# Attention scores of an encoder trunk: the rotary product on 128 partitions with the chunk mask in it, and output-projection products between the last attention steps

## What is computed

```python
q = jnp.concatenate([q[..., :NOPE_DIM],
                     apply_rope(q[..., NOPE_DIM:], cos[:, :, None, :], sin[:, :, None, :])], axis=-1)
...
def attend(args):
    qb, qc = args
    s = jnp.einsum('bqhd,bkhd->bhqk', qb, k).astype(jnp.float32) * scale
    mask = k_chunk[None, :] <= qc[:, None]
    s = jnp.where(mask[None, None], s, neg)
    p = jax.nn.softmax(s, axis=-1).astype(v.dtype)
    return jnp.einsum('bhqk,bkhd->bqhd', p, v)
...
return o @ w_o
```

## Time and profile before

| | us |
|---|---|
| median of 3 runs | 1961.33 (1961.1 to 1962.72) |
| span of the profiled execution, first to last instruction | 1960.5 |
| PE busy in it | 1873.7 (96%) |
| DVE busy | 998.9 (51%) |
| ACT busy | 590.6 (30%) |
| POOL busy | 266.5 (14%) |
| mean granted clock of PE, share of full speed | 0.973 |

### The profile page before, as it was taken

How to read it: one execution, slowest core, us unless ns; L and a number is a source line. 1 busy time by engine, 2 the same in 40 slices (tenths; PEclk the granted TensorE clock), 3 DMA queues, 4 the chain that set the end, 5 groups by cost and what they waited for, 6 DMA issues and landing times.

```text
span 1960.5 us, 22646 instructions
## 1 busy us (share of the span) xinstructions
PE 1873.7 (96%) x8196; PEld 1494.7 (76%) x8196; DVE 998.9 (51%) x1306; ACT 590.6 (30%) x794; POOL 266.5 (14%) x171
## 2 busy tenths in 40 slices
PE   8887999998999999999999999999899999999996
PEld 5665887785888888888878888888655778888885
DVE  7889358725645544442285444323744354444224
ACT  5122222222233332331153323212424342323213
POOL 7456105301301300000020000000200100000001
PEclk8999999999999999999999999999969999999998
DMA  4244425565632222222222222222100122222221
GB/s 161 92 142 139 137 97 164 152 250 176 195 123 96 97 96 96 96 97 96 97 86 96 96 96 96 97 97 96 65 22 1 65 97 96 96 96 96 97 96 54
DMA packets 79398, 207.93 MB, mean 106 GB/s; under 512 B 24576, under 2 KB 32896, under 8 KB 77296
## 3 DMA queue, kind: packets, MB, share of 16 engines
q1 hardware_dynamic: 75440, 187.86, 28.5%
q0 software_dynamic: 2752, 17.24, 2.6%
q10 hardware_dynamic: 1152, 2.10, 0.3%
HBM read 184.10 MB, written 23.07 MB: 106 GB/s over the span
## 4 chain that ended last, share of the span: by engine, by line
PE 80%; DVE 12%; issue 4%; ACT 2%; POOL 1%; DMA 0%; DVEq 0%; SPq 0%; ACTq 0%; POOLq 0%
PE bank L1356 24%; PE bank L1358 24%; PE bank L1357 23%; DVE w_split L912 2%; PE bank L1670 1%; PE bank L1669 1%; DVE h_split L932 1%; PE bank L1691 1%; ACT w_split L604 1%; DVE gate L925 1%; PE bank L1552 1%; PE bank L1559 1%; PE bank L1673 1%; PE bank L1388 1%; PE bank L1682 1%
## 5 line engine op out<-in xcount | busy, mean ns | idle before, releaser
L912 DVE TENSOR_TENSOR w_split<-w_raw,w_split 128x1024 fp32r<-128x1024 f32 x302 | 390.5, 1297 | 684.2 <-ACT w_split L604 679.0
L1356 PE MATMUL bank<-h_split,w_split 128*128 128x512 f32 x1488 | 586.4, 394 | 21.2 <-DVE gate L923 13.3
L1357 PE MATMUL bank<-h_split,w_split 128*128 128x512 f32 x1488 | 581.5, 391 | 0.0
L1358 PE MATMUL bank<-h_split,w_split 128*128 128x512 f32 x1488 | 581.3, 391 | 0.0
L604 ACT ACTIVATE w_split<-w_raw 128x1024 fp32r<-128x1024 f32 x302 | 316.5, 1055 | 723.7 <-PE bank L1358 719.7
L1356 PEld LDWEIGHTS bank<-h_split,w_split 128*128 128x128 f32 x1488 | 281.1, 189 | 87.8 <-DVE gate L923 11.9
L1356 PE MATMUL bank<-g_split,w_split 128*128 128x512 f32 (+1 forms) x856 | 335.8, 392 | 7.0 <-DVE gate L923 3.6
L1357 PE MATMUL bank<-g_split,w_split 128*128 128x512 f32 (+1 forms) x856 | 334.7, 391 | 0.0
L1358 PE MATMUL bank<-g_split,w_split 128*128 128x512 f32 (+1 forms) x856 | 334.5, 391 | 0.0
L1358 PEld LDWEIGHTS bank<-h_split,w_split 128*128 128x128 f32 x1488 | 280.8, 189 | 59.1
L1357 PEld LDWEIGHTS bank<-h_split,w_split 128*128 128x128 f32 x1488 | 281.0, 189 | 58.8 <-issue 1.0
(11 more groups left out here) (243 smaller groups left out, 1254.2 us busy)
## 6 DMA issues: line engine op xcount, KB each, us to landing
w_raw<-wstream SPq DMA_DIRECT2D x302, 512.0 KB, 3.2
op_slots<-s_ops POOLq DMA_DIRECT2D x5, 2048.0 KB, 8.3
s_ops<-ops_out SPq DMA_DIRECT2D x8, 1024.0 KB, 4.4
op_slots<-s_ops SPq DMA_DIRECT2D x3, 2048.0 KB, 8.3
s_ops<-c_pow POOLq DMA_DIRECT2D x8, 512.0 KB, 4.2
s_ops<-k_window SPq DMA_DIRECT2D x64, 64.0 KB, 3.3
x_res<-xT SPq DMA_DIRECT2D x8, 256.0 KB, 8.2
bc_in<-bcd POOLq DMA_DIRECT2D x8, 256.0 KB, 5.5
```

The costliest lines, as they stand in the source:

```text
L912: tt(W[:, r, 1, :], RAW[:, r, :], W[:, r, 0, :].bitcast(F32), ALU.subtract).then_inc(s_lo, 1)
L1356: mm(bank, hi, x_hi, start=start, stop=True, skip_group_check=True)
L1357: mm(bank, hi, x_lo, start=False, stop=True, skip_group_check=True)
L1358: return mm(bank, lo, x_hi, start=False, stop=True, skip_group_check=True)
```

## The change

The kernel after contracts all 128 partitions in the rotary product. The query tile, now `q_rope_and_rows`, has a place of its own for each of the 8 heads: one half of the partitions holds the head's rotary queries, the other half holds four rows that are 1 for the first 64 queries of tile t (and 60 rows of zeros). The key side has two tiles: `k_rope` for even heads and the former `c_kv` for odd ones (`KRP`), with the rotary key in one half and in the other four rows of -3e38 at the keys to be hidden. So L1673 falls away. POOL loads these rows with four transfers from a new 2 x 64 x 512 input and copies half of the key once. The product that ended with the mask now ends a step. DVE writes the rotary queries with two additions of 64 partitions in place of one of 128. The probabilities lie packed in 1280 columns per head. At the end of the attention, the first three projection packs are multiplied by heads 0 to 5 ahead of and between the last turns, and by heads 6 and 7 behind `values(7)`.

```diff
-                tt(QR[:, q, :], BK[ea % 8][:], COS[:], ALU.mult).then_inc(s_ev_v, 1)
+                tt(ACC[:], BK[ea % 8][:], COS[:], ALU.mult).then_inc(s_ev_v, 1)
                 wait_product(dve, eb)
                 tt(GT[:], BK[eb % 8][:], SIN[:], ALU.mult).then_inc(s_ev_v, 1)
                 wait_read(dve, eb)
-                tt(QR[:, q, :], QR[:, q, :], GT[:], ALU.add).then_inc(s_qr, 1)
-                dve.wait_ge(s_qr, q + 1)
+                for par in range(2):
+                    side = slice(64 * par, 64 * par + 64)
+                    tt(QR[side, 2 * q + par, :], ACC[side, :], GT[side, :], ALU.add).then_inc(s_qr, 1)
+                dve.wait_ge(s_qr, 2 * q + 2)
...
             sum_squares(N_KV)
+            pool.wait_ge(s_used, FFN1A + 3 * FT)
+            for par in range(2):
+                side = slice(64 * (1 - par), 64 * (1 - par) + 64)
+                pool.dma_start(QR[side, par:HEADS:2, :], mask[0].unsqueeze(1).broadcast_to([64, HEADS // 2, SEQ])
+                               ).then_inc(s_rows, 16)
             sum_squares(N_DQ)
+            pool.wait_ge(s_cs_lo, 1)
+            pool.wait_ge(s_sum, (SUMS[N_DQ] + 1) * (DT - 1))
+            nc.gpsimd.tensor_copy(CN[64:P, :], KR[64:P, :]).then_inc(s_kro, 1)
+            pool.wait_ge(s_kro, 1)
+            for par in range(2):
+                side = slice(64 * (1 - par), 64 * (1 - par) + 64)
+                pool.dma_start(KRP[par][side, :], mask[1]).then_inc(s_rows, 16)
...
-            pe.wait_ge(s_qr, 4)
+            pe.wait_ge(s_qr, HEADS)
+            pe.wait_ge(s_rows, 16 * 4)
...
                 n = P * (t + 1)
-                q0 = 64 * (h % 2)
                 mm(BK[t][:, 0:n], QN[:, h, t * P:(t + 1) * P], KN[:, h, 0:n], start=True, stop=True, skip_group_check=True)
-                mm(BK[t][:, 0:n], QR[q0:q0 + 64, h // 2, t * P:(t + 1) * P], KR[q0:q0 + 64, 0:n],
-                   start=False, stop=True, skip_group_check=True)
-
-                mm(BK[t][:, n - 64:n], MASK[0:1, 0:P], MASK[0:1, P:P + 64], start=False, stop=True,
+
+                mm(BK[t][:, 0:n], QR[:, h, t * P:(t + 1) * P], KRP[h % 2][:, 0:n], start=False, stop=True,
                    skip_group_check=True).then_inc(s_scores, 1)
...
-            for h in range(HEADS + 2):
+            def wo_part(d, heads):
+                for k in heads:
+                    pe.wait_ge(s_o_lo, k + 1)
+                    last = three(BK[d][:], *tile(WO + d, k), H[:, k, 0, :], H[:, k, 1, :], k == 0)
+                return last
+
+            for h in range(HEADS):
                 for t in range(4):
-                    if h < HEADS:
-                        scores(h, t)
-                    if 1 <= h <= HEADS:
+                    scores(h, t)
+                    if h >= 1:
                         turn(h - 1, t)
                     if t == 1 and h >= 2:
                         values(h - 2)
-            for d in range(DT):
+            early, last_two = range(HEADS - 2), range(HEADS - 2, HEADS)
+            values(HEADS - 2)
+            for d in range(AHEAD):
                 pack(WO + d)
-                if d in (4, 6, 7):
-
-                    pe.wait_ge(s_o_lo, HEADS)
-                column(WO + d, BK[d], H, (lambda k: pe.wait_ge(s_o_lo, k + 1)) if d == 0 else None)
+                pe.wait_ge(s_exp, 4 * (HEADS - 1) + d + 1)
+                wo_part(d, early)
+                if d < 2:
+                    turn(HEADS - 1, 2 * d)
+                    turn(HEADS - 1, 2 * d + 1)
+            values(HEADS - 1)
+            for d in range(AHEAD):
+                wo_part(d, last_two).then_inc(s_used, 1)
+            for d in range(AHEAD, DT):
+                pack(WO + d)
+                if d == 3:
+                    pe.wait_ge(s_exp, 4 * HEADS)
+                if d in (4, 5):
+                    pe.wait_ge(s_pt, 4 * HEADS)
+                column(WO + d, BK[d], H)
```

More of the change, by code:

```diff
@@ L135, in build @@
     EYE = at("eye", [P, P], F32, o_c + 800)
-    MASK = at("mask_rows", [1, P + 64], F32, o_c + 1312)
     STAT = at("attn_stat", [P, 32], F32, o_c + 2080)
@@ L190, in build @@
     QN = at("q_nope", [P, HEADS, SEQ], F32, o_g + 32 * K)
-    QR = at("q_rope", [P, 4, SEQ], F32, o_g + 48 * K)
-    PT = at("probs_t", [P, 2, 4, SEQ], F32, o_g + 56 * K)
-    PR = at("probs", [P, 2, 4, SEQ], F32, o_g + 72 * K)
+    QR = at("q_rope_and_rows", [P, HEADS, SEQ], F32, o_g + 48 * K)
+    PT = at("probs_t", [P, 2, 4, SEQ], F32, o_g + 64 * K)
+    PR = [at("probs_even", [P, 1280], F32, o_g + 80 * K), at("probs_odd", [P, 1280], F32, o_s + 2 * K)]
+    PR_AT = [0, 128, 384, 768]
+    KRP = [KR, CN]
     CS = at("c_kv_split", [P, 2, SEQ], F32R, o_g + 72 * K)
@@ L316, in wait_read @@
             eng.wait_ge(s_ev_v, [MSTAT, *range(MCQ, MID)].index(m) + 1)
-    CONSTS = 4
+    CONSTS = 3
     def in_turns(eng, stage, turn):
@@ L372, in reduced, with probs @@
         return ts(to_cos, to_cos, float(np.pi / 2), None, ALU.add)
+    def probs(h, t, first, end):
+        return PR[h % 2][:, PR_AT[t] + first:PR_AT[t] + end]
     with nc.Block() as block:
@@ L515, in _ @@
             pool.dma_start(EYE[:], consts[1]).then_inc(s_const, 16)
-            pool.dma_start(MASK[:], mask).then_inc(s_const, 16)
             pool.dma_start(DS[:], dskip).then_inc(s_const, 16)
@@ L844, in soft @@
                     act.wait_ge(s_tp, i - 7)
-                nc.scalar.activation(PR[:, h % 2, t, 0:n], BK[t][:, 0:n], ACT.Exp, bias=STAT[:, 4 + t:5 + t],
+                nc.scalar.activation(probs(h, t, 0, n), BK[t][:, 0:n], ACT.Exp, bias=STAT[:, 4 + t:5 + t],
                                      scale=QK_SCALE, accum_out=STAT[:, 8 + t:9 + t]).then_inc(s_exp, 1)
@@ L1681, in turn @@
                 for a in range(t + 1):
-                    last = nc.tensor.transpose(BK[4 + t % 2][:, a * P:(a + 1) * P],
-                                               PR[:, h % 2, t, a * P:(a + 1) * P], EYE[:])
+                    last = nc.tensor.transpose(BK[4 + t % 2][:, a * P:(a + 1) * P], probs(h, t, a * P, (a + 1) * P), EYE[:])
                 last.then_inc(s_tp, 1)
@@ L1779 @@
     consts = np.stack([np.ones((P, P), f), eye, np.roll(eye, 64, 0)])
-    mask = np.concatenate([np.repeat([1.0, 0.0], 64), np.full(64, NEG)]).astype(f)[None]
+    mask = np.zeros((2, 64, SEQ), f)
+    for t in range(4):
+        mask[0, t, t * P:t * P + 64] = 1.0
+        mask[1, t, t * P + 64:(t + 1) * P] = NEG
     def states(v):
```

4 lines of the change are left out of this document (2 added, 2 removed).

## The result

The kernel after takes **1937.77 us** (median of 4 runs, 1933.79 to 1937.82) against 1961.63 for the kernel before (4 runs beside them): a ratio of **0.9877**, 95% interval 0.9865 to 0.9889, 23.9 us faster. The forecast was 1932.4 in a range of 1927 to 1941.

The account below looks back on a forecast made before the run. PE, busy for 96% of the 1960.5 us span, was taken to bound the kernel. Terms 2.4 - 19.8 + 3.7 - 15.1 - 0.1 = -28.9 us gave 1931.6 from the span, 1932.4 from the median; range 1927 to 1941.

Parts of the forecast that it names:

- Term 1: Start of the scores: two 64-partition DVE additions replace one, 4 more operations at 0.60 us, +2.4 us.
- Term 2: Score steps: mask product and delays around products on few partitions go from 32 steps, -19.8 us.
- Term 3: Score loop: with shorter steps PE waits for ACT's copy of turned probabilities, in six heads and head 1, +3.7 us.
- Term 4: PE's clock in heads 0 to 2: low for about 5 us instead of through most of them, -15.1 us.
- Term 5: Tail from last scores to projection: new waits of 1.95 and 0.9 us replace 2.95 us of waits, -0.1 us.
- Cost nothing: POOL's row transfers, its key copy and one small load fewer at the start: no effect on the time.
- The delays stay: Rival, score steps: delays come from new accumulation or unhidden weight loads, not changing partitions; 1939 us, chance 0.12.
- The clock comes back late: Rival, first heads: scores don't raise the clock, half speed up to and with head 2's first values; 1944 us, chance 0.08.
- The clock low throughout: Rival: half clock through the whole score loop, to the first projection product; 1988 us, slower than before, chance 0.02.
- The softmax becomes the bound: Rival, score loop: the softmax chain is late by another microsecond in seven heads, +7; 1939 us, chance 0.06.
- PE's first score released by the mask rows: Sign of a wrong forecast at the first score: PE waits there for the mask rows instead of DVE.

Follow-up runs that it names:

- turn_later: Kernel after with each head's second turn and the values behind it moved behind the third scores instead of the second; 1931.22 us, ratio 0.9855.
- no_mask: Kernel before without its mask product (L1673), so the chunk mask is left out; 1940.59 us, ratio 0.9898.
- third_product: Kernel after with a one-partition product of 64 columns, adding zeros, at the end of each score step; 1948.64 us, ratio 0.9937.
- tail_only: Kernel before with only the loops at the end of the attention as the kernel after has them; 1961.37 us, ratio 1.0004.
- copy_by_dma: Kernel after with POOL's copy of half the rotary key made a transfer, and it and two mask-row transfers moved behind L600; 1933.94 us, ratio 0.9859.
- all_four: all_three plus the edit of turn_later, on the kernel after; POOL's transfers stand behind its four rotary additions; 1931.25 us, ratio 0.9854.
- after_again: Kernel after, unchanged, run again to see how its runs spread; 1936.70 us, ratio 0.9876.
- all_three: Kernel after with copy_by_dma's and pool_adds' edits, plus tail products reordered to cover the waits at the values of heads 6 and 7; 1934.99 us, ratio 0.9874.
- pool_adds: Kernel after with the odd head's rotary addition of each pair moved from DVE to POOL, products double-buffered; 1932.99 us, ratio 0.9852.
- scores_only: Kernel after with its new scores, but the end of the attention as in the kernel before; 1935.51 us, ratio 0.9863.

## Why the prediction was right, point by point

The forecast's mechanism held, the sign and the range too; the time was 5.3 us above the point. Two of its terms were each off by 2 us or more in opposite directions, which the sum hides.

- **Term 1** (+2.4) was mis-sized. Two 64-partition additions do cost as much as two of 128, but a pair of heads got 0.72 us longer, not 0.60: the second addition starts 0.72 us behind the first, as if it depended on it, though neither reads what the other writes. Why, no run shows. That is the upper bound, 2.9; PE's idle time grew by 2.99, to 5.22, outside the 4.4 to 4.8 that were to show the forecast right.
- **Term 2** (-19.8) was mis-sized: -22.3, beyond its own bound of -20.8. A head without a wait takes 7.57 us (turn_later), 2.82 less than 10.39. The steps follow at the pure stream, 0.86 and 0.22, so the whole 0.65 went from each of the 32 steps (-20.8), and the 0.03 left per step for a boundary don't exist. The rest, 1.5 us, is the 0.05 per turn that the forecast kept in its 1.31 us for the turns of a head. no_mask shows the mask's 0.36 go whole. By the Trainium skill (TensorE: Matmul & The Clock Gate, Back-to-back issue gap) the masks would be 1.6 us in all, by the prediction's estimate. no_mask alone gained 20.8 us by the medians, 11.5 of them by the row and most of the rest, 8.5, by the clock that came back 17 us earlier (an estimate: half of 17). (The prediction's -10.9 for the term by that figure leaves out the 1.0 it left for boundaries.)
- **Term 3** (+3.7) was mis-sized: the waits, 0.97 in head 1 and 0.57 in six heads, show as 4.4 us, but cost 5.7 by the starts, 1.13 in head 1 and 0.76 in each other. The reading of ACT's chain gave 0.45, taken as 0.5, and 0.7. turn_later confirms whose wait the 0.57 was. Terms 2 and 3 together came to -16.6 for -16.1: that the score stretch agrees to a tenth is luck.
- **Term 4** (-15.1): head 0 took 7.17 us for 4.32 at full clock (four steps of two products at 0.216 per 128 columns), so 2.85 for the 2.5 forecast: -14.8. The clock came back 5.6 us behind the first score, in head 0, for the 5 forecast. The reason was read too narrowly, though: `values` isn't what raises the clock, since it came back ahead of any `values` in no_mask and third_product too.
- **Term 5** (-0.1) **failed**: +1.57, outside its bounds of -2.0 and +1. The two waits came as forecast, 1.99 for 1.95 and 0.72 for 0.9, and tail_only measured -0.18 for the same code. What was left out is that the clock may fall behind a wait of 2 us: `values(6)` alone took 1.14 us more. The forecast had noted that 2.23 us of idle time ahead of the scores were followed by a fall, and did not apply it to the wait it was adding itself.
- **"Cost nothing" failed in part**: POOL's addition L600 was on time, as said, but its copy and the two transfers run beside DVE's splits, which take 0.4 us longer with them, and a second clock fall, behind the norm product's wait, came with it. The stretch to the first score lost 2.0 us beyond term 1. copy_by_dma moves the fall and does not prove its cause.
- **The rivals.** "The delays stay" is ruled out by third_product. "The clock comes back late" did not happen in after; no_mask (20.5 us) and third_product (17) show that it does with products on fewer partitions. The clock low throughout did not come. "The softmax becomes the bound" is true of one wait per head (0.57, or 0.76 by the starts), not of a microsecond more.
- **PE's first score released by the mask rows**, given as a sign of error, did not occur in after, but all_four produced it by the order on POOL.

The three errors, 0.6 in term 1, 2.0 ahead of the scores and 1.7 in the tail, make 4.3 of the 5.3 us, and the last 1.0 lies within what the medians differ by from one group of runs to the next; after_again, against the runs of before beside it, gained 24.65 us, and 28.9 less 4.3 is 24.6.

## What to carry to other kernels

Short float32 products on few partitions can cost more by the delays around them than by their columns (0.36 us a mask for 0.11 of stream), and kernels with them got TensorE's full clock back 10 to 32 us later; fold what they add into spare partitions of a product that is needed anyway. For every wait that a change adds on TensorE, even of 2 us, ask what stands behind it and whether that would run at half clock; in the tail, covering two waits, 2.7 us together, was worth 4.9. Where transfers share a queue with compute, put each at the place where its data is ready, not where the code for it happened to be added. And size a wait by the starts around it in a kernel without it: the idle time shown was up to 0.2 us short each time.

## What the runs showed of the hardware

- Around float32 products on fewer than 128 partitions: 0.10 us ahead of one of 64 or 1 partitions, 0.19 behind one of 64, 0.25 behind one of 1, and 0.05 more in the turn that follows (0.49 for 0.44 with four transpositions); 0 between products of 128.
- From the first score to the return of the full clock: 3.3 to 6.1 us in ten profiles with 128-partition products alone, 15.9 with a one-partition product in each step, 20.9 with a 64-partition one, 38 with both. The low clock itself lasted 3.4 to 13.7 us in the ten, the longest where PE waited 11.3 us for the first score (all_three).
- Waits of 1.99 us (the tail of after, after_again, pool_adds and copy_by_dma) and of 2.03 to 2.09 (the norm product of after and five others) were followed by a fall; waits of 1.88 and 1.21 (scores_only), 1.84 (tail_only) and 1.66 (the norm product before) were not. But turn_later waits 2.00 in the tail without one (`values` in 2.39), so the wait's length alone does not decide.
- On POOL an addition of 64 x 512 takes 1.77 us where DVE takes 0.68. Two such additions on DVE start 0.72 us apart, though neither needs the other.
